# First mixer of the second block: compressed scores and first softmax scores inside the last two value projections

## What is computed

```python
proj = x @ w_in
qa, kc, vc, ksl, vsl, kw, vw, ga, qm, km, vm = jnp.split(proj, EVEN_SPLITS, axis=-1)
qa, kc, ksl, kw = rope(qa), rope(kc), rope(ksl), rope(kw)        # also qm, km
kc, vc = compress(kc, ...), compress(vc, ...)                     # 15 compressed keys
s_c = jnp.einsum('bqkgd,bnkd->bkgqn', qb, kc) * scale             # "compressed scores"
p_c = masked_softmax(s_c, cmp_end[None, :] <= t[:, None])
o_c = jnp.einsum('bkgqn,bnkd->bqkgd', p_c, vc)
s_s, s_w = scores with the selected and with the window keys
p_s, p_w = masked_softmax(s_s, m_s), masked_softmax(s_w, m_w)
o = gb[..., 0:1] * o_c + gb[..., 1:2] * o_s + gb[..., 2:3] * o_w
o_b = moba_attention(rope(qm), rope(km), vm)
return jnp.concatenate([o_a, o_b], axis=-1) @ w_out
```

## Time and profile before

| | us |
|---|---|
| median of three executions | 1573.45 |
| lowest, highest | 1571.62, 1573.88 |
| the profiled execution, its time | 1572.79 |
| the profiled execution, its span | 1571.0 |
| TensorE busy in the span | 1411.9 (90%) |
| VectorE busy in the span | 1193.0 (76%) |
| ScalarE busy in the span | 483.1 (31%) |
| mean granted TensorE clock | 0.955 |

### The profile page before, as it was taken

One profiled execution on the slowest core, in us unless ns is written; L12 is line 12 of the kernel. 1 busy time (PEld: TensorE's weight loads), 2 busy tenths in 40 slices (PEclk: granted clock), 3 DMA queues, 4 the chain that ended last, 5 costly groups with the idle time before them and its releaser, 6 DMA issues.

```text
span 1571.0 us, 23870 instructions
## 1 busy us (share of the span) xinstructions
PE 1411.9 (90%) x9796; PEld 1280.4 (82%) x9796; DVE 1193.0 (76%) x1517; ACT 483.1 (31%) x812; POOL 23.2 (1%) x49
## 2 busy tenths in 40 slices
PE   6899999997899999998999889988779888899885
PEld 5889889997889989998996788876669777797664
DVE  6798799686798899686668876777576688667775
ACT  3422320123222320122016141266210553315641
POOL 0000100000000000001000000000000000000000
PEclk9999999998999999998998999999979998999998
DMA  6434744533434534435440334598635214358870
GB/s 235 140 105 159 254 135 145 178 115 118 156 109 161 198 125 161 161 110 182 135 161 1 108 135 137 189 302 284 213 125 181 98 56 147 117 168 273 286 267 27
DMA packets 205963, 249.72 MB, mean 159 GB/s; under 512 B 5738, under 2 KB 191210, under 8 KB 205856
## 3 DMA queue, kind: packets, MB, share of 16 engines
q1 hardware_dynamic: 199968, 226.61, 43.9%
q0 software_dynamic: 5072, 18.73, 3.3%
q10 hardware_dynamic: 816, 2.87, 0.5%
HBM read 246.09 MB, written 2.10 MB: 158 GB/s over the span
## 4 chain that ended last, share of the span: by engine, by line
PE 57%; DVE 25%; ACT 7%; DMA 6%; issue 3%; SPq 0%; DVEq 0%; ACTq 0%
PE bank L435 37%; DVE wL L1723 8%; DMA ring<-in_moe_w_up 6%; PE bank L1009 4%; PE bank L630 3%; DVE wH L1721 3%; ACT wH L1582 3%; DVE proj L1896 2%; PE bank L953 1%; DVE work L1915 1%; PE bank L748 1%; PE bank L466 1%; DVE work L1950 1%; PE bank L990 1%; PE bank L454 1%
## 5 line engine op out<-in xcount | busy, mean ns | idle before, releaser
L435 PE MATMUL bank<-hH,wH 128*128 128x256 f32 x1648 | 485.7, 295 | 33.7 <-DVE wL L1723 17.6
L435 PE MATMUL bank<-hL,wH 128*128 128x256 f32 x1648 | 474.3, 288 | 0.0
L435 PE MATMUL bank<-hH,wL 128*128 128x256 f32 x1648 | 473.8, 288 | 0.0
L1723 DVE TENSOR_TENSOR wL<-ring,wH 128x2048 fp32r<-128x2048 f32 x184 | 419.8, 2281 | 41.3 <-ACT wH L1582 36.2
L435 PEld LDWEIGHTS bank<-hH,wH 128*128 128x128 f32 x1648 | 324.7, 197 | 44.9 <-DVE wL L1723 37.7
L435 PEld LDWEIGHTS bank<-hL,wH 128*128 128x128 f32 x1648 | 324.9, 197 | 0.7
L435 PEld LDWEIGHTS bank<-hH,wL 128*128 128x128 f32 x1648 | 324.3, 197 | 0.0
L1721 DVE CAST wH<-ring 128x2048 fp32r<-128x2048 f32 x138 | 168.5, 1221 | 40.7 <-PE bank L435 29.7
L435 PE MATMUL bank<-wH,hH 128*128 128x256 f32 (+1 forms) x400 | 114.7, 287 | 3.1 <-DVE hL L2071 3.1
L435 PE MATMUL bank<-wL,hH 128*128 128x256 f32 (+1 forms) x400 | 113.0, 283 | 0.0
L435 PE MATMUL bank<-wH,hL 128*128 128x256 f32 (+1 forms) x400 | 113.0, 283 | 0.0
(11 more groups left out here) (438 smaller groups left out, 2165.0 us busy)
## 6 DMA issues: line engine op xcount, KB each, us to landing
ring<-in_w_gate SPq DMA_DIRECT2D x40, 1024.0 KB, 5.2
ring<-in_w_in SPq DMA_DIRECT2D x34, 1024.0 KB, 5.3
ring<-in_moe_w_down SPq DMA_DIRECT2D x32, 1024.0 KB, 4.9
ring<-in_moe_w_gate SPq DMA_DIRECT2D x40, 512.0 KB, 4.0
ring<-in_moe_w_up SPq DMA_DIRECT2D x40, 512.0 KB, 5.1
ring<-in_moe_w_gate SPq DMA_DIRECT2D x12, 1024.0 KB, 5.4
ring<-in_moe_w_up SPq DMA_DIRECT2D x12, 1024.0 KB, 5.6
ring<-in_sb_w_in SPq DMA_DIRECT2D x12, 1024.0 KB, 5.1
```

What stands on the lines that cost most here:

```text
L435: last = mm(ps[:, m * CW:m * CW + (width if token_major else S)], a, b, start=k == 0 and i == 0, stop=k == KT - 1 and i == 2)
L1723: tt(low, raw_w, high, ALU.subtract).then_inc(split_ready, 1)
```

## The change

The two groups of compressed scores become a function, `compressed_scores(par)`. The first is called between the halves of ("vm", 0), the second behind ("vm", 0) and ahead of `turned(8)`. The scores of softmaxes 0 and 1 are made between the halves of ("vm", 1), and the loop leaves them out. The wait for all rotations (`roped`) is replaced by waits for those that each group reads: 3, 5, and all of them only before the first MoBA scores.

```diff
-            for c in range(2):
-                columns(("vm", c), [rows8(w_ab, o_vm + c * CW, CW)], True)
-                if c == 0:
-                    turned(len(ropes))
-
-            eng.wait_ge(*emptied_at("kcc"))
-            eng.wait_ge(roped, len(ropes) + 1)
-            for par in range(2):
-                ps = open_bank(eng, ("cl", par))
...
+            def compressed_scores(par):
+
+                if par == 0:
+                    eng.wait_ge(*emptied_at("kcc"))
+                    eng.wait_ge(roped, 3)
+                ps = open_bank(eng, ("cl", par))
+                r0 = par * HD
+                for g in range(NSA_H // 2):
+                    for t in range(T):
+                        c = (2 * g + t) * 16
+                        kv = g // 2
+                        last = mm(ps[:, c:c + NC_], QA[r0:r0 + HD, g * S + t * P:g * S + (t + 1) * P],
+                                  kcc[r0:r0 + HD, kv * NC_:(kv + 1) * NC_], start=True, stop=True)
+                last.then_inc(*fills(("cl", par)))
+
+            def first_scores():
+
+                eng.wait_ge(roped, 5)
+                full_qk(0)
+
+            columns(("vm", 0), [rows8(w_ab, o_vm, CW)], True, mid=lambda: compressed_scores(0))
+            compressed_scores(1)
+            turned(len(ropes))
+            columns(("vm", 1), [rows8(w_ab, o_vm + CW, CW)], True, mid=first_scores)
             for i in range(0, len(SOFT) + 6, 2):
-                if i < len(SOFT):
+                if i == 2 * NSA_H:
+                    eng.wait_ge(roped, len(ropes) + 1)
+                if 0 < i < len(SOFT):
                     full_qk(i)
```

## The result

| | kernel before | changed kernel |
|---|---|---|
| median, us | 1572.72 (20 runs) | 1576.26 (20 runs) |
| lowest, highest | 1568.10, 1574.72 | 1571.16, 1579.65 |
| ratio, 95% interval | | 1.0023 [1.0014, 1.0032] |
| profiled execution, time and span | 1572.79, 1571.0 | 1578.28, 1576.5 |
| mean granted clock | 0.955 | 0.954 |

The change costs 3.5 us, between 2.2 and 5.0: slower, by just more than the 3.1 us that I had called the least that can be told. The forecast's side is right and its time, 1575.2, is 1.1 us short; what came is nearest to rival B, 1577.2. A part of that nearness is luck: the forecast stood on a median of three executions, 1573.45, and twenty gave 1572.72. As a difference it was 1.7 us against 3.5.

What follows compares the result with a forecast made beforehand. It saw a TensorE stall before `LC` at low clock, then VectorE setting the pace until 864.92. Sum: -1.4 (`LC` earlier) + 3.1 (split) + 0 (low clock) = +1.7 us on the 1573.45 median, 1575.2; range 1571.0 to 1578.5.

Steps and rivals of the forecast that it cites:

- rival B: Behind VectorE's late split, 2.3 us TensorE gap (heads 14, 15) brings second clock fall: +3.7 us, 1577.2; chance 0.15.
- (4): Before the transposes of `LC`: ScalarE's copy of ("vm", 1) delays its exponentials; TensorE still resumes 1.4 us earlier.
- (5): VectorE's split of ("mix", 0) moves from idle time into its pace-setting stretch: price 3.1 to 3.55 us, taken as 3.1.
- (6): Ahead of `LC`, a 3.0 us TensorE gap brings the clock fall about 5 us later; VectorE's waits stay: 0.
- (1): Compressed scores, 3.2 us, stay on TensorE's path, 1.6 inside ("vm", 0) and 1.6 behind it; moving saves nothing.
- (2): First softmax scores inside ("vm", 1) run at full clock, 1.8 instead of 3.3 us; ("vm", 1) ends 5.0 us later.
- (3): Last key pair's turn comes 3.2 us later; VectorE's compressed additions and maxima are done by 818.3; no cost.
- the two gaps of the earlier trace: TensorE gaps: 2.85 us before 943.00 with a clock fall, 2.11 before 955.74 without; so 3.0 should bring one.
- Rival A: Softmax steps run at full clock, VectorE's waits of 0.80, 2.45 and 0.18 go: -1.7 us, 1571.7; chance 0.23.
- Rival C: Clock falls earlier, inside the projections, in ("vm", 1), after narrow records: about +3.7 us, 1577.2; chance 0.10.

Runs made afterwards that it cites:

- e1: Changed kernel with VectorE's split of the ("mix", 0) weights put back ahead of the last rotation; 1572.47 us, 0.9998 of the kernel before.
- e2: Kernel before, scores unmoved, with VectorE's split of the ("mix", 0) weights late, at the first `split_bank`; 1579.39 us, 1.0041.
- e9: Changed kernel with 13 overwritten matmuls ahead of the scores of heads 12 and 13, while VectorE splits; 1576.86 us, 1.002 of the kernel before.
- e10: Changed kernel with ScalarE's copy of ("vm", 1) behind the first exponentials, plus 13 matmuls ahead of the scores of heads 12 and 13; 1570.35 us, 0.9988.
- e6: Changed kernel with the first scores back behind ("vm", 1), only the compressed scores moved, and the split early; 1568.82 us, 0.9984 of the kernel before.
- e3: Changed kernel with ScalarE's copy of ("vm", 1) behind the first exponentials instead of ahead of them; 1572.62 us, 1.0002 of the kernel before.
- e4: Changed kernel with 20 dense, overwritten matmuls in TensorE's pause before the transposes of `LC`; 1572.83 us, 1.001 of the kernel before.
- e5: Changed kernel with the split back ahead of the last rotation and ScalarE's copy of ("vm", 1) behind the first exponentials; 1566.09 us, 0.9966.
- e11: Kernel before with only ScalarE's copy of ("vm", 1) put behind its first exponentials; 1572.01 us, 0.9995.
- e7: Changed kernel with all compressed scores behind ("vm", 1) in one piece, so only the first scores moved; 1572.17 us, 1.0005 of the kernel before.
- e12: Changed kernel with only the compressed scores moved, split early, and ScalarE's copy of ("vm", 1) behind the first exponentials; 1569.19 us, 0.9984.
- e8: Kernel before with seven dense, overwritten matmuls in its 1.5 us pause ahead of the transposes of `LC`; 1569.41 us, 0.9984.

## Why the prediction came out as it did

The sum had +1.7 us; the profiled stage has +3.4 and the medians +3.5. By its steps:

| step | predicted | measured |
|---|---|---|
| (4) `LC` earlier | -1.4 | 22.98 - 23.84 = -0.9 |
| (5) the split | +3.1 | +3.5 |
| (6) waits behind the first fall | 0 | 3.81 - 3.43 = +0.4 |
| (rival B) waits behind a second fall | 0 | +0.4 |
| sum | +1.7 | +3.4 |

**(1), (2), (4).** The first scores took 1.8 us at full clock, as said. The narrow groups were mis-sized: I had 1.6 us each from 2.92 us for 29 records; they cost 1.88 from the start of one to what follows it at 812.06, and together with the seams L673 comes 4.05 us later behind the mark, not 3.2. ScalarE's copy is the last link, as step (4) had it, and the chain from it to `LC` took 4.2 us, where my times made 4.7. Net 0.9 us gained instead of 1.4.

**(3).** Right: VectorE was done with the compressed additions and maxima long before 824 and waited 4.35 us for ScalarE.

**(5).** The mechanism was right, and e1, e2, e9 and e10 show it from four sides. The size was off by 0.4: I let the later wait of 0.42 before 864.92 absorb part of it, and it is still there at 869.44. I read this so: the wait isn't slack that a late VectorE eats, since TensorE itself depends on VectorE's pace in this stretch and shifts with it. No run tests that reading.

**(6).** Right that the first fall moves from 818 into the pause; the pause was 2.46 us, not 3.0. The rise came at 840, 13 us behind the resumption at 826.88, where before it was 12.3 (826.63 to 838.9), and the wait of 2.45 became 2.84. Two reasons given for this step don't hold in general. The products with the values don't bring the rise (e6). And the two gaps of the earlier trace rows don't make a limit between 2.11 and 2.85 us, as the last section shows: that the first fall came was likely, not certain. The page "TensorE: Matmul & The Clock Gate" of the Trainium skill (section "The HAM clock gate"), by which steady matmul activity lifts the low level, would have it back soon after 826.88; the row of 838 to 840 shows 2.00 of 2.00 us busy and 0.50 granted.

**Rival A** didn't come in the median, but its condition is real: in e3, e4 and e5, where the pause is filled or gone, the clock stays up behind `LC` (in e3 and e4 until the pause behind the split). e5 has 2.7 us less of waits than e1, and `LC` 2.6 earlier. **Rival C** did not come. **Rival B**, which I gave 0.15, is what happened: the pause of 2.34 us and the fall behind it. Its named wait was one step off: what is held up is not the scores of heads 14 and 15 but the transposes of head 8, which need the bank that `split_bank` empties (released by L2273 in the row at 850.69). Its price I put at 2; it was 0.4 in the profiled execution and 3.5 in those of e2 and e3. The time was near B's because B's 2 covered what the forecast's terms lacked.

So the step that failed is no single one: each term of the sum was short by 0.4 or 0.5 us in the same direction, and the second fall, another 0.4, was left to a rival. The mechanism of the forecast, the split's new place, is what e1 and e2 show.

## What to carry to other kernels

When a call is moved that other engines use as their clock ("one more than what was asked for until here"), look first at where the work that hangs on it lands: here 3.5 us of VectorE went from a wait into its busiest stretch, and one argument put them back. Moving a producer forward is worth nothing while an unrelated copy stands ahead of its consumer on another engine: with both groups of scores moved, the late copy gained 5 us (e1 to e5), where the late copy alone (e11) and the moved first scores alone (e6 to e1) gave none. A pause of TensorE can cost more than its length when the clock falls behind it: filling one of 2.46 us, with `LC` at the same place, took 3.6 us off the profiled stage (e4).

## What the hardware showed that I had not expected

- In this stage, TensorE's pauses of 2.34 to 2.71 us at full clock were each followed by 1.2 GHz, and those of 0.75 and 1.10 weren't. Over the whole traces of the fourteen kernels the line isn't sharp. Of 51 pauses between 2.3 and 2.9 us at full clock, 48 had the fall in them or up to 1.5 us behind them; of 29 between 2.0 and 2.3 us it was 2, of 47 between 1.7 and 2.0 us it was 8. The very pause of 2.85 us of the earlier trace rows, behind which the clock reads 0.50 from 942 to 946 in the kernel before, has 1.00 from 938 to 948 in e11. So the length of a pause doesn't decide by itself; what else does stays open.
- Once low, the level came back after very different times of the same kind of work. From TensorE's resumption, in the softmax steps, it was about 3 us (changed kernel, behind 850.69, and e4), 6 (e6, behind 826.02), 9.4 to 11 (e1, e2 behind its split, e3, e7, e12), 12 (before, e11) and 13 (e9, and the changed kernel behind 826.88). In e8 TensorE had no pause at all in the low stretch and stayed at 1.2 GHz from 816.1 to 833.1. What decides it stays open; with it stays open why three of the changed kernel's 20 executions took 1571.2 to 1571.6 us, at a mean clock of 0.964 to 0.966 where the profiled one had 0.954. The kernel before scatters likewise: 3 of its 20 executions took less than 1570 us.
- The same steps that don't raise the level hold it: 1.00 over more than 40 us in e5.
- The medians and the profiled stages don't agree to better than 1 to 2 us. The stages of e1, e5 and e10 gain more (1.8, 7.1 and 3.8 us against 0.3, 5.3 and 1.9 by the ratios), those of e8 and e12 less (1.6 and 1.7 against 2.5). One profile each can't tell whether the stage differs in other executions or the rest of the program does.
